# In-projection groups 7 to 15 of the second half with seven block products and ready-made weight parts

## What is computed

```python
for l in range(DEPTH):                                     # 2
    h = _rmsnorm(x, norm_gain[l])
    proj = jnp.einsum('bsd,de->bse', h, w_in[l])           # 2048 x 4352, the in-projection
    q, k, v, g_attn, x_rnn, g_rnn = jnp.split(proj, splits, axis=-1)
    attn = _swa_sink_attention(q, k, v, sinks[l], cos, sin)   # window 128, 16 heads of 64
    xc = _causal_conv(x_rnn, conv_w[l], conv_b[l])
    rnn = _rg_lru(xc, w_rgate[l], b_rgate[l], w_igate[l], b_igate[l], lru_param[l])
    mixed = jnp.concatenate([attn * jax.nn.silu(g_attn), rnn * jax.nn.silu(g_rnn)], axis=-1)
    x = x + jnp.einsum('bse,ed->bsd', mixed, w_out[l])     # 2048 x 2048, the out-projection
return _rmsnorm(x, final_gain)
```

## Time and profile before

| | |
|---|---|
| median of 3 runs | 2303.87 us (2301.64 to 2306.47) |
| profiled execution | 2304.23 us, its span 2301.7 us |
| TensorE busy | 2292.8 us of the span, granted clock 1.00 |
| DVE, ACT busy | 1565.0 us, 1339.1 us |
| DMA | 287.48 MB moved, mean 125 GB/s |

### The profile page before, as it was taken

How to read it: one execution, slowest core, us unless ns; L and a number is a source line. 1 busy time by engine, 2 the same in 40 slices (tenths; PEclk the granted TensorE clock), 3 DMA queues, 4 the chain that set the end, 5 groups by cost and what they waited for, 6 DMA issues and landing times.

```text
span 2301.7 us, 36298 instructions
## 1 busy us (share of the span) xinstructions
PE 2292.8 (100%) x13798; PEld 1919.3 (83%) x13798; DVE 1565.0 (68%) x2546; ACT 1339.1 (58%) x2564; POOL 32.3 (1%) x58
## 2 busy tenths in 40 slices
PE   9999999999999999999999999999999999999999
PEld 8877888899888888889888888888988888888898
DVE  7658868656646877856675786885565478778555
ACT  7557666445546857645564676763455557666444
POOL 1110000000000000000000000000000000000000
PEclk9999999999999999999999999999999999999999
DMA  8886334545333233344534333344543333333444
GB/s 259 237 243 174 88 92 120 152 138 139 96 93 98 86 89 92 96 145 139 163 110 152 111 95 89 96 139 138 142 131 96 97 91 86 93 92 96 117 136 152
DMA packets 141389, 287.48 MB, mean 125 GB/s; under 512 B 16416, under 2 KB 20768, under 8 KB 138784
## 3 DMA queue, kind: packets, MB, share of 16 engines
q1 hardware_dynamic: 138096, 259.91, 38.1%
q0 software_dynamic: 2688, 25.17, 4.5%
q10 hardware_dynamic: 432, 0.10, 0.0%
HBM read 276.73 MB, written 33.55 MB: 135 GB/s over the span
## 4 chain that ended last, share of the span: by engine, by line
PE 96%; DVE 2%; DMA 1%; ACT 1%; issue 0%; DVEq 0%; POOL 0%; ACTq 0%; POOLq 0%
PE proj L682 80%; PE proj L703 10%; PE ps_at L811 2%; DMA wall<-in_w 1%; PE ps_at L786 1%; PE ps_at L830 1%; PE proj L722 1%; ACT wcut L905 0%; DVE wcut L1307 0%; PE proj L749 0%; PE ps_at L640 0%; DVE mixed L1791 0%; DVE acc L1402 0%; ACT operand L942 0%; PE ps_at L764 0%
## 5 line engine op out<-in xcount | busy, mean ns | idle before, releaser
L682 PE MATMUL proj<-operand,wcut 128*128 128x512 f32 x8376 | 1944.0, 391 | 1.3 <-DVE xr L1558 1.3
L682 PEld LDWEIGHTS proj<-operand,wcut 128*128 128x128 f32 x8376 | 1563.7, 188 | 337.9 <-issue 10.3
L1307 DVE TENSOR_TENSOR wcut<-wall,wcut 128x512 fp32r<-128x512 f32 x871 | 600.1, 689 | 582.0 <-ACT wcut L905 575.1
L905 ACT ACTIVATE wcut<-wall 128x512 fp32r<-128x512 f32 x870 | 548.3, 630 | 547.2 <-DMA wall<-in_w 381.0
L703 PE MATMUL proj<-xsum_out,wcut 128*128 128x256 f32 x1104 | 136.8, 283 | 0.0
L703 PEld LDWEIGHTS proj<-xsum_out,wcut 128*128 128x128 f32 x1104 | 134.9, 192 | 0.6
L703 PEld LDWEIGHTS proj<-operand,wcut 128*128 128x128 f32 x828 | 105.3, 191 | 3.9 <-DVE proj L1371 0.3
L703 PE MATMUL proj<-operand,wcut 128*128 128x256 f32 x828 | 106.6, 283 | 0.0
L1011 ACT ACTIVATE gy<-proj 32x512 f32<-32x512 f32 x144 | 85.1, 591 | 26.6 <-PE proj L682 22.1
L1102 ACT ACTIVATE sqr<-ps_at,pars 64x512 f32<-64x512 f32 x64 | 43.9, 685 | 91.8 <-PE ps_at L830 91.4
L1063 ACT ACTIVATE prob<-ps_at,stat 128x128 f32<-128x128 f32 x256 | 90.1, 363 | 0.8
(11 more groups left out here) (173 smaller groups left out, 1520.6 us busy)
## 6 DMA issues: line engine op xcount, KB each, us to landing
wall<-in_w SPq DMA_DIRECT2D x710, 256.0 KB, 2.6
wall<-weight_sums SPq DMA_DIRECT2D x92, 256.0 KB, 2.7
weight_sums<-in_blocks POOLq DMA_DIRECT2D x36, 512.0 KB, 6.5
wall<-in_blocks SPq DMA_DIRECT2D x69, 256.0 KB, 2.6
x<-in_xt SPq DMA_DIRECT2D x16, 512.0 KB, 3.8
mixed<-in_xt SPq DMA_DIRECT2D x14, 512.0 KB, 6.7
weight_sums<-weight_sums POOLq DMA_DIRECT2D x12, 512.0 KB, 5.2
gw<-in_gates SPq DMA_DIRECT2D x32, 128.0 KB, 2.6
```

The source lines that it names most:

```text
L682: last = pe.matmul(bank_of(l, 2 * g + m)[:, :], wcut[:, n % RING, a, c:c + P], operand[:, k, b, :], start=(i == 0 and k == 0), stop=(k == ...
L905: act.activation(wcut[:, u % RING, 0, :], wall[:, u % RING, 1, :], ACT.Copy).then_inc(w_hi, 1)
L1307: dve.tensor_tensor(wcut[:, u % RING, 1, :], wall[:, u % RING, 1, :], wcut[:, u % RING, 0, :].bitcast(F32), ALU.subtract).then_inc(w_lo, 1)
```

## The change

In the second half of the tokens (`h` = 1) the in-projection groups 7 to 15 of both layers use seven products. In the first half the same groups read their weights in blocks (`block` units, 12 matmuls of 128 x 512 as before), and seven of their eight split units are stored to HBM with both parts (`weight_cuts`, 512 KB each, 126 in all). In the second half the units whose parts were stored (`READY`, seven of the eleven in a group) are loaded from there straight into `wcut`, with no work of ACT or DVE; TensorE waits for the load itself. The four weight sums of a group are loaded and split as before. SP issues the store of unit u + 2 at the beat of u, after DVE has split it, and before it loads over a stored unit it waits for its store. In the last layer of the second half x is kept in HBM (`x_kept`) while its place holds the operand sums.

POOL has 16 batches instead of 6. `OPENS` parts them: batches 0 and 1 at the start, batches 2 to 8 from slot 132 of the first layer of the first half on, batches 9 to 15 from slot 132 of its second layer on.

```diff
-IN_SEVEN = {(0, 0): (), (0, 1): (), (1, 0): (), (1, 1): ()}
+IN_SEVEN = {(0, 0): (), (0, 1): (), (1, 0): range(7, IN_LAST + 1), (1, 1): range(7, IN_LAST + 1)}
...
-CUT_AT, READY, STORED = {}, set(), []
-SPLIT_NO = {n: n + 1 for n in range(TOTAL + UPG - RING)}
+KEYS = []
+CUT_AT = {}
+for n, (h, l, kind, g, j) in enumerate(UNIT):
+    if h == 0 and zone_of(g) == "in" and g in BUILT[l] and (kind, j) != ("block", WHOLE[A21]):
+        CUT_AT[key_of(l, kind, g, j)] = n
+        KEYS.append(key_of(l, kind, g, j))
+READY = {n for n, (h, l, *unit) in enumerate(UNIT) if h > 0 and key_of(l, *unit) in CUT_AT}
+STORED = sorted(CUT_AT.values())
+SPLIT = [n for n in range(TOTAL + UPG - RING) if n not in READY]
+SPLIT_NO = {n: i + 1 for i, n in enumerate(SPLIT)}
...
+OPENS = {2: (0, 0, 132), 9: (0, 1, 132)}
...
+                if n in READY:
+                    from_n = CUT_AT[key_of(l, kind, g, j)]
+                    sp_.wait_ge(cut_out[from_n % RING], 16 * stores_through(from_n))
+                    sp_.dma_start(wcut[:, n % RING, :, :].rearrange("p a c -> p (a c)").bitcast(F32),
+                                  cuts[KEYS.index(key_of(l, kind, g, j))]).then_inc(w_in[n % RING], 16)
+                    return
...
                                 sp_.wait_ge(unit_done, u + 1)
+                                if u in STORED:
+                                    sp_.wait_ge(cut_out[u % RING], 16 * stores_through(u))
                                 w_load(u + RING)
+                            if u + 2 in STORED:
+
+                                sp_.wait_ge(w_lo, SPLIT_NO[u + 2])
+                                sp_.dma_start(cuts[KEYS.index(key_of(l, *UNIT[u + 2][2:]))],
+                                              wcut[:, (u + 2) % RING, :, :].rearrange("p a c -> p (a c)").bitcast(F32)
+                                              ).then_inc(cut_out[(u + 2) % RING], 16)
...
+                if n in OPENS:
+                    pool.wait_ge(built[S4], 32 * n - 16)
+                    add(S4, n - 1, A12)
+                    pool.wait_ge(unit_done, at_unit(*OPENS[n]))
...
-                pe.wait_ge(w_lo, SPLIT_NO[n])
+                if n in READY:
+                    pe.wait_ge(w_in[n % RING], 16 * (n // RING + 1))
+                else:
+                    pe.wait_ge(w_lo, SPLIT_NO[n])
```

More of the change, by code:

```diff
@@ L168, with stores_through @@
 BATCH.sort(key=lambda batch: batch[1] < PG)
-CUT_AT, READY, STORED = {}, set(), []
-SPLIT_NO = {n: n + 1 for n in range(TOTAL + UPG - RING)}
+KEYS = []
[8 more added lines that the diff above has]
+SPLIT_NO = {n: i + 1 for i, n in enumerate(SPLIT)}
 X_BACK = [(h, l) for h in range(HALVES) for l in range(DEPTH) if l == 0 or (h, l, "in") in ZONES]
+def stores_through(n):
+    return sum(m % RING == n % RING for m in STORED if m <= n)
 def tile_of(what, t):
@@ L294, in build @@
         x_kept = nc.dram_tensor("x_kept", (4, P, KT // 4 * TOK), F32).ap()
+        cuts = nc.dram_tensor("weight_cuts", (len(KEYS), P, 2 * KU * GW), F32).ap()
         rout = mu
@@ L320, in build @@
         built = {n: sem(f"built{n}") for n in SUMS}
+        cut_out = [sem(f"cut_out{i}") for i in range(RING)]
         kept = [sem(f"kept{i}") for i in range(4)]
@@ L622, in _ @@
                     add(S3, n, A21)
-                if before:
+                if before and n not in OPENS:
                     pool.wait_ge(built[S4], 32 * n - 16)
```

## The result

The change makes the kernel slower: 2328.42 us median (2326.6 to 2334.06, 4 runs) against 2302.76 us (2301.56 to 2306.47, 4 runs), a ratio of 1.0113, 95% interval 1.0091 to 1.0135. The prediction was 2306.6 us in a range of 2290 to 2323: the time lies outside it. The place and the kind of the loss were forecast, but the one term that was called decisive was sized at less than half.

The account below looks back on a forecast made before the run. TensorE, busy 2292.8 of 2301.7 us, was taken as the bound, so only matmuls and its waits count. 2304.2 - 13.9 (matmuls) - 2.7 (early attention) + 18 (sums beside out-projections) + 1 (small waits) = 2306.6 us, range 2290 to 2323.

Parts of the forecast that it names:

- the one term that was called decisive: First half's out-projections, both layers: weight sums built by POOL beside seven-product groups delay weight loads; 18 us added, ends 0 and 35.
- The early relief: First layer's attention, first half: with only two batches at the start, sums no longer run beside it; 2.7 us saved.
- The stores: First half: 126 transfers of 512 KB out of `wcut` cost nothing, ends 0 and +5 us.
- Matmuls: 18 groups: 864 matmuls of 512 columns replaced by 1,512 of 256; 13.9 us saved, 0.77 for each group.
- The forecast +1 for small waits in the second half: Second half's groups: attention and recurrence with DVE 79% busy not free of small waits; +1 us, ends -1 and +9.
- Added: 2 layers x 4.4 x 2.0 = 18 us: First half's out-projections: 4.4 batches of sums in each layer, each delaying TensorE by 2.0 us through late weight loads.
- the tightest allowance: Seven-product groups: the unit with least time lets its weight load take 5.5 us to land before TensorE waits.
- Rival B: First half, slots 148 to 199, both layers: DMA engines over-asked, queue not emptying between bursts, 4 us a batch; 2324, chance 0.20.
- C: Second half, beside attention: DVE's lead sums come late, TensorE waits 1 us x 18; 2324 us, chance 0.09.
- Rival A: First half's out-projections: sums hardly hold up loads, landings near the median of 5.7 us; 2291 us, chance 0.28.
- D: First half, groups 7 to 15: stores hold up SP and all loads, 5 to 10 us on top; 2314, chance 0.05.
- E: Seven-product groups: the change does not do what it says, no shorter groups; 2320 us, chance 0.02.

Follow-up runs that it names:

- e1: The changed kernel with its sums opened at other places, none beside a seven-product out-projection group of the first half: 2289.89 us against 2303.51 before.

## Why the prediction was wrong

**Right.** The early relief: 2.7 forecast, 2.8 measured. The stores: nothing forecast, nothing measured (a DMA share of 0.8 at 235 GB/s forecast, 0.71 at 230 measured). The sums beside the first half's out-projections decide, with waits between 444 and 570 and between 1014 and 1139, as the trace shows. About half of that idle time is on `wcut` itself, most of the rest on the lead sum that stands behind a late split. The forecast sum lay above the time before, but by too little to call it slower, and only 0.36 stood on slower; the direction was not forecast.

**Matmuls: -13.9 forecast, -16.7 measured**, 0.93 for a group instead of 0.77. TensorE's timeline at the starts of two groups' first wide stretches, beside attention in the second half:

```profile
1380.99 5.63 PE L719 MATMUL proj<-operand,wcut 128*128 128x512 f32 x24
...
1405.47 5.63 PE L719 MATMUL proj<-operand,wcut 128*128 128x512 f32 x24
```

The distance is 24.48 us; before it was 25.43 (chain pieces at 1308.27 and 1333.70). The 0.1204 us of a narrow matmul came from groups without attention; what the other 0.16 is was not tried. The forecast +1 for small waits in the second half did not show: no wait of TensorE after 1160 us.

**The step that failed is "Added: 2 layers x 4.4 x 2.0 = 18 us".** Measured: 42.6 us, or 4.8 for each batch, beyond even the upper end of 4. Three things were mis-sized:

1. The overrun was averaged as if a batch delayed one burst of three loads, with landings of 9.3, 8.3 and 7.3 us. The earlier trace rows already had 8.0, 8.8 and 10.9 for three such loads. In the trace of after, the landings of loads issued in 434 to 440, 462 to 468 and 492 to 496 go up to 9.4, 10.1 and 9.8, with medians of 8.8, 8.0 and 9.6. With a load every 1.9 us instead of 2.7, more of them are in the way of each row: of the 59 loads issued in 440 to 570 us, 33 took over 5.5 us, the tightest allowance, about seven for a batch in place of three. The median was 6.0.
2. The clock was left out. It fell to 1.2 GHz in or after four waits (2.3 to 8.2 us long), and the matmuls there took 8.2 us longer.
3. The x loads in front of a weight load at slot 148 of the second layer, in SP's own order, were not priced. I knew them from SP's list and had no term for them. What they cost is not settled by the run that spread them.

**Rival B** gave 2324, with C the nearest number, but its reason is refuted: at a DMA share of 0.88 the loss is nearly gone when accumulating transfers come one by one, and at 0.79 two thirds of it stay when they come in rows of three. Nor did the queue stay full between the rows: a load issued at 478.6 landed after 2.7 us. The medians of 6.0 and 5.7 stayed under its 7. **Rival A** (2291) was wrong for the change as made. The Trainium skill (DMA: Bandwidth & Descriptors, section Queues, rings and completion order) has each DMA engine go round robin between its queue rows, a whole packet of descriptors at a time. The trace speaks against the rival that was drawn from that rule: beside the sums a load took up to 10.9 us to land, and 15.7 behind the x loads. In which order the engines took the packets no run here shows. **C** did not occur: its sign, waits of late units on lead sums, did show, but in the first half and behind late loads. **D** did not, **E** did not.

The range failed because the bounds of the decisive term were those of an average over one assumed burst. The early stretch showed that a landing can take 10.9 us; a load late by 5.4 us in each of 8.8 batches would have been 48 us, an end that the rows allowed and that I had reduced by reckoning.

## What to carry to other kernels

Background transfers are placed by the slack of what they delay, not by the mean DMA share. Beside plain groups with 13.6 us from issue to use they cost little: TensorE was never idle in 400 to 440 us of the changed kernel, at a share of 0.95, and the early stretch of the kernel before lost 2.8 us. Beside groups with 7.0 to 11.0 us (the prediction's allowances and 1.5 us for the splits) they cost 4.8 us a batch, at a share of 0.93 and 0.90. If they must run there, issue them one at a time. That bought back 34 us, of which the slower pace of the sums alone would have given about 12. Cutting them into small pieces bought back as much, but it also spread the issues, so what the size does by itself stays open. Check on the issuing engine's timeline that an edit changed only what it was meant to change. And price a wait of several microseconds on TensorE at more than its length, because the clock can fall behind it.

## What was not expected of the hardware

- Three accumulating transfers issued within 3 us held other loads up by far more than the same transfers one at a time: landings up to 10.9 us against 7.9 in 440 to 600 us. With the sums at about the same pace (16.6 and 17.8 MB in that stretch) it is 22 us of the kernel's time, 2316.2 against 2294.4, though the rows of three had the lower DMA share (0.79 against 0.88).
- With pieces of 2 KB instead of 8 KB, POOL issued each accumulating transfer of a row only when the one before had landed (7.0 and 8.4 us apart in the row shown; large ones all went out within 3 us). Why is not shown.
- The clock did not follow the length of a wait. The wait of 2.94 us that ended at 505.47 was followed by time at 1.2 GHz (0.66 as the mean of 505 to 510, first row below), and so were waits of 2.86 and 2.26 us (0.57 in 1079 to 1087, 0.66 in 1130 to 1135). One of 3.57 us was not: the 36 wide matmuls behind it take 8.40 us (second row), as at full clock. What decides it stays open.

```profile
505.00:510.00 5.00, 4.53 (x25) 4.53 (x26) 4.34 (x8) 3.32 (x7) 0.77 (x1) 0.66 0.76 271
```

```profile
535.02 8.40 PE L719 MATMUL proj<-operand,wcut 128*128 128x512 f32 x36 [3.57 <-DVE wcut L1344]
```

- 126 stores of 512 KB from `wcut` landed in 3.9 us each (median) and left the time of their stretch unchanged to the last digit (569.59 us in e1), at 230 GB/s and a DMA share of 0.71 in 740 to 960 us of the changed kernel.
